# Expert weights in DMA rows of 16 KB, each transfer filling two neighbouring slots of the weight ring

## The reference

```python
logits = xf @ w_router + b_router                    # 32 experts
top_v, top_e = lax.top_k(logits, 4)
gates = softmax(top_v)
# for each expert e, for the tokens that chose it:
gu = xb @ w_e1[e] + b_e1[e]                          # w_e1[e]: 1024 x 2048
g, u = gu[:, :1024], gu[:, 1024:]
g = minimum(g, 7.0); u = clip(u, -7.0, 7.0)
h = (u + 1.0) * (g * sigmoid(1.702 * g))
y = h @ w_e2[e] + b_e2[e]                            # w_e2[e]: 1024 x 1024
# weighted by the gates and added to the token's row; then residual and final RMSNorm
```

## Time and profile before

| what | value |
|---|---|
| median of 3 runs | 1271.91 us (1271.19 to 1272.47) |
| the profiled execution's own time | 1270.08 us |
| its span, first to last instruction | 1267.8 us |
| mean granted TensorE clock | 0.979 |
| PE busy in the span | 1165.9 us (92%) |
| bytes moved in the span | 457.40 MB, mean 361 GB/s |

### The profile page before, as it was taken

One profiled execution on the slowest core, in us unless ns is written; L12 is line 12 of the kernel. 1 busy time (PEld: TensorE's weight loads), 2 busy tenths in 40 slices (PEclk: granted clock), 3 DMA queues, 4 the chain that ended last, 5 costly groups with the idle time before them and its releaser, 6 DMA issues.

```text
span 1267.8 us, 15137 instructions
## 1 busy us (share of the span) xinstructions
PE 1165.9 (92%) x5540; PEld 567.2 (45%) x5540; DVE 338.3 (27%) x820; ACT 182.1 (14%) x354; POOL 27.7 (2%) x54
## 2 busy tenths in 40 slices
PE   8999999698899999999989898989999999999896
PEld 6888888386333343333333333323332323233332
DVE  3795424614122122021212121211202021212123
ACT  3114213203010111111010101111010111010102
POOL 4000001100000000000000000000000000000000
PEclk9999999888999999999999999999999999999999
DMA  9398333993799999999999999999999999999994
GB/s 302 91 289 274 137 102 132 362 419 115 278 390 416 421 422 422 421 422 422 421 422 422 421 422 422 421 422 421 421 421 422 420 422 422 421 422 422 421 422 168
DMA packets 92741, 457.40 MB, mean 361 GB/s; under 512 B 7827, under 2 KB 36715, under 8 KB 44069
## 3 DMA queue, kind: packets, MB, share of 16 engines
q1 hardware_dynamic: 90768, 452.27, 88.8%
q10 hardware_dynamic: 1117, 3.04, 0.6%
q0 software_dynamic: 832, 1.76, 0.5%
HBM read 453.71 MB, written 3.81 MB: 361 GB/s over the span
## 4 chain that ended last, share of the span: by engine, by line
PE 51%; DMA 24%; SPq 14%; DVE 6%; issue 3%; ACT 2%; ACTq 0%; POOL 0%; DVEq 0%
DMA ring<-in_w_e 23%; PE ps L1539 15%; SPq L353 12%; PE ps L1559 12%; PE ps L1250 11%; PE ps L1269 3%; DVE ring L955 2%; PE ps L1501 1%; PE ps L1510 1%; PE ps L1549 1%; SPq L361 1%; PE ps L1453 1%; DVE mix L1106 1%; DVE mix L1109 1%; DVE mix L1103 1%
## 5 line engine op out<-in xcount | busy, mean ns | idle before, releaser
L1539 PE MATMUL ps<-ring,mix 128*64 128x512 f32 x2016 | 457.5, 598 | 28.9 <-DMA ring<-in_w_e 27.6
L1539 PEld LDWEIGHTS ps<-ring,mix 128*64 128x64 f32 x2016 | 134.1, 136 | 336.8 <-issue 234.8
L1559 PE MATMUL ps<-ring,mix 128*64 128x512 f32 x1024 | 235.1, 613 | 22.0 <-issue 11.0
L1103 DVE TENSOR_SCALAR mix<-ps 128x512 f32<-128x512 f32 x32 | 22.1, 692 | 606.7 <-PE ps L1539 606.7
L1559 PEld LDWEIGHTS ps<-ring,mix 128*64 128x64 f32 x1024 | 79.5, 140 | 156.0 <-issue 142.0
L686 ACT ACTIVATE mix<-mix 128x512 f32<-128x512 f32 x32 | 20.1, 630 | 420.3 <-DVE mix L1103 420.3
L1510 PEld LDWEIGHTS ps<-mix 128*128 128x128 f32 x544 | 65.5, 198 | 14.4 <-issue 13.0
L1510 PE MATMUL ps<-mix 128*128 128x128 f32 x544 | 70.1, 284 | 1.3 <-ACT rstd L668 1.3
L696 ACT ACTIVATE mix<-ps 64x512 f32<-64x512 f32 x64 | 37.8, 591 | 227.1 <-PE ps L1559 226.8
L1090 DVE SCALAR_TENSOR_TENSOR mix<-mix,gates 128x1024 f32<-128x1024 f32 x16 | 20.5, 1284 | 154.8 <-ACT mix L696 154.8
L1250 PE MATMUL ps<-mix,ring 128*128 128x264 f32 x256 | 60.2, 400 | 0.3 <-ACT mix L639 0.3
(11 more groups left out here) (294 smaller groups left out, 651.6 us busy)
## 6 DMA issues: line engine op xcount, KB each, us to landing
ring<-in_w_e SPq DMA_DIRECT2D x380, 1024.0 KB, 25.0
ring<-in_w_in SPq DMA_DIRECT2D x8, 1024.0 KB, 15.7
ring<-in_cache_mem_k SPq DMA_DIRECT2D x8, 1024.0 KB, 4.9
ring<-in_cache_mem_v SPq DMA_DIRECT2D x8, 1024.0 KB, 8.3
ring<-in_w_k SPq DMA_DIRECT2D x4, 1024.0 KB, 8.9
ring<-in_w_v SPq DMA_DIRECT2D x4, 1024.0 KB, 12.7
ring<-in_w_out SPq DMA_DIRECT2D x4, 1024.0 KB, 12.5
ring<-in_w_q SPq DMA_DIRECT2D x4, 1024.0 KB, 12.0
```

The source lines that it names most:

```text
L1103: dve.tensor_scalar(g1, ps[0][:, :], LIMIT, None, ALU.min).then_inc(S["g_clamped"], 1)
L1539: m = pe.matmul(ps[gu][CAP * i:CAP * i + CAP, :], xeT[:, k, CAP * e2:CAP * e2 + CAP], g_u[gu][:, 512 * i:512 * i + 512], start=False, stop ...
L1559: m = pe.matmul(ps[3][CAP * i:CAP * i + CAP, :], hTv[:, k % 4, CAP * (k // 4):CAP * (k // 4) + CAP], ring[:, s, D * (k % 2) + 512 * i:D * ...
```

## The change

Each transfer of expert weights now covers two neighbouring slots: 2 MB, 128 rows of 16 KB. To make a row of 16 KB out of `w_e1`, a partition takes two neighbouring rows of it (2p and 2p+1 of a block of 256), of which one comes to lie in slot s and the other in slot s+1; for `w_e2` it takes four. `fill` is called for every second slot and waits until both slots are freed; one semaphore, that of the even slot, stands for both. On the other side `DEAL[k]`, a slice with step 2, picks the token columns that match slot k, in `gather`, in the transposes of the sample tokens and in `fill_head`; `turn_h` picks every fourth column of h instead of every second. No arithmetic is added or taken away.

```diff
--- before.py
+++ after.py
@@ -76,6 +76,7 @@
 assert MOE0 % RING == 0
 HEAD_SLOTS = W_SLOTS // 2
 KC_SLOTS = 8
+DEAL = [slice(2 * P * (_k // 2) + _k % 2, 2 * P * (_k // 2 + 1), 2) for _k in range(KD)]
 
 
 IN_ORDER = [4, 5, 6, 7, 0, 1, 2, 3]
@@ -343,19 +344,18 @@
 
                 sp.wait_ge(S["freed"], free)
                 if s < W_SLOTS:
-                    src = a["w_e1"][0][bass.ds(e, 1), s * P:(s + 1) * P, :].rearrange("o p c -> p (o c)")
-                    dst = ring[:, s, :]
+                    src = a["w_e1"][0][bass.ds(e, 1), s * P:(s + 2) * P, :].rearrange("o (p t) c -> p (o t c)", t=2)
                 else:
                     j = s - W_SLOTS
-                    src = a["w_e2"][0][bass.ds(e, 1), j * 2 * P:(j + 1) * 2 * P, :].rearrange(
-                        "o (p t) c -> p (o t c)", t=2)
-                    dst = ring[:, s, :]
+                    src = a["w_e2"][0][bass.ds(e, 1), j * 2 * P:(j + 2) * 2 * P, :].rearrange(
+                        "o (p t) c -> p (o t c)", t=4)
+                dst = ring[:, s:s + 2, :].rearrange("p s c -> p (s c)")
                 sp.dma_start(dst, src).then_inc(filled[s], 16)
 
             def expert(e, b, first=0):
 
-                for s in range(first, RING):
-                    fill(e, s, RING * b + freed_after(MOE0 + s - RING))
+                for s in range(first, RING, 2):
+                    fill(e, s, RING * b + freed_after(MOE0 + s + 1 - RING))
 
             def bias(e):
                 sp.dma_start(b1q[0:97:32, :], a["b_e1"][0][bass.ds(e, 1), :].rearrange("o (g c) -> (o g) c", g=4)).then_inc(
@@ -363,7 +363,7 @@
 
             def fill_head(k):
                 for gu in range(2):
-                    sp.dma_start(head[k][gu], a["w_e1"][0, 0, k * P:(k + 1) * P, D * gu:D * gu + D]).then_inc(S["head_filled"], 16)
+                    sp.dma_start(head[k][gu], a["w_e1"][0, 0, DEAL[k], D * gu:D * gu + D]).then_inc(S["head_filled"], 16)
 
 
             sp.wait_ge(S["freed"], freed_after(KV_ENTRY[7]))
@@ -371,20 +371,20 @@
             sp.wait_ge(S["score_done"], H)
             fill_head(1)
             fill_head(2)
-            for s in range(HEAD_SLOTS, W_SLOTS):
-                fill(0, s, freed_after(MOE0 + s - RING))
+            for s in range(HEAD_SLOTS, W_SLOTS, 2):
+                fill(0, s, freed_after(MOE0 + s + 1 - RING))
             bias(0)
-            for s in range(HEAD_SLOTS):
-                fill(1, s, freed_after(MOE0 + s - RING))
-            for s in range(W_SLOTS, RING):
-                fill(0, s, freed_after(MOE0 + s - RING))
+            for s in range(0, HEAD_SLOTS, 2):
+                fill(1, s, freed_after(MOE0 + s + 1 - RING))
+            for s in range(W_SLOTS, RING, 2):
+                fill(0, s, freed_after(MOE0 + s + 1 - RING))
             sp.wait_ge(S["tm_turned"], 6)
             fill_head(3)
             sp.wait_ge(S["b1_used"], 1)
             bias(1)
 
-            for s in range(HEAD_SLOTS, W_SLOTS):
-                fill(1, s, freed_after(MOE0 + 2 * (s - HEAD_SLOTS)))
+            for s in range(HEAD_SLOTS, W_SLOTS, 2):
+                fill(1, s, freed_after(MOE0 + 2 * (s + 1 - HEAD_SLOTS)))
             expert(1, 1, W_SLOTS)
             with sp.Fori(2, NE) as e:
                 sp.wait_ge(S["b1_used"], e)
@@ -1507,7 +1507,7 @@
                 for i in halves:
                     for k in range(4 * i, 4 * i + 4):
                         for t in range(2):
-                            m = pe.matmul(ps[4 + i][:, P * (k % 4):P * (k % 4) + P], xnt[:, t, k * P:(k + 1) * P],
+                            m = pe.matmul(ps[4 + i][:, P * (k % 4):P * (k % 4) + P], xnt[:, t, DEAL[k]],
                                           sel[:, t, :], start=(t == 0), stop=(t == 1))
                 if halves[-1] == 1:
                     m.then_inc(S["gathered"], 1)
@@ -1531,9 +1531,9 @@
                         pe.wait_ge(S["head_filled"], 2 * 16 * HEAD_SLOTS)
                         g_u = head[k]
                     elif k < HEAD_SLOTS:
-                        pe.wait_ge(filled[k], 16 * b + 16 * (fills_before(MOE0 + k) - 1))
+                        pe.wait_ge(filled[k - k % 2], 16 * b + 16 * (fills_before(MOE0 + k) - 1))
                     else:
-                        pe.wait_ge(filled[k], 16 * b + 16 * fills_before(MOE0 + k))
+                        pe.wait_ge(filled[k - k % 2], 16 * b + 16 * fills_before(MOE0 + k))
                     for gu in range(2):
                         for i in range(2):
                             m = pe.matmul(ps[gu][CAP * i:CAP * i + CAP, :], xeT[:, k, CAP * e2:CAP * e2 + CAP],
@@ -1545,15 +1545,14 @@
             def turn_h(b):
                 pe.wait_ge(S["h_ready"], b + 1)
                 for j in range(4):
-                    c = 2 * P * (j // 2) + j % 2
-                    m = pe.transpose(ps[2][:, j * P:(j + 1) * P], hh[:, c:c + 2 * P - 1:2], ident[:, :])
+                    m = pe.transpose(ps[2][:, j * P:(j + 1) * P], hh[:, j:4 * P:4], ident[:, :])
                 m.then_inc(S["h_turned"], 1)
 
             def down(b):
                 pe.wait_ge(S["hT_ready"], b + 1)
                 for k in range(KD):
                     s = W_SLOTS + k // 2
-                    if k % 2 == 0:
+                    if k % 4 == 0:
                         pe.wait_ge(filled[s], 16 * b + 16 * fills_before(MOE0 + s))
                     for i in range(2):
                         m = pe.matmul(ps[3][CAP * i:CAP * i + CAP, :], hTv[:, k % 4, CAP * (k // 4):CAP * (k // 4) + CAP],
@@ -1600,7 +1599,7 @@
 
             pe.wait_ge(S["xnt_kept"], 6)
             for k in range(KD):
-                m = pe.transpose(ps[2][:, NB * k:NB * k + NB], xnt[0:NB, 2, k * P:(k + 1) * P], ident[0:NB, 0:NB])
+                m = pe.transpose(ps[2][:, NB * k:NB * k + NB], xnt[0:NB, 2, DEAL[k]], ident[0:NB, 0:NB])
             m.then_inc(S["smp_chain"], 1)
             pe.wait_ge(S["gt0_kept"], 1)
             gather(0)
```

## The result

| | before | after |
|---|---|---|
| median of 5 runs | 1271.19 us (1269.91 to 1272.47) | 1261.19 us (1260.38 to 1264.40) |
| the profiled execution's own time | 1270.08 us | 1263.79 us |
| its span | 1267.8 us | 1261.4 us |

The ratio is 0.9931, with a 95% interval from 0.9917 to 0.9944: 8.8 us less, 7.1 to 10.6 (the medians themselves are 10.0 apart). The forecast was 9.3 less, 1262.6.

What follows compares the result with a forecast made beforehand. The DMA engines, full from about 380 us, were taken as the bound, not PE. Rows -12.7, start +1.7 and end +1.7 gave -9.3 us, a median forecast of 1262.6 us, range 1258.5 to 1268.5.

Steps and rivals of the forecast that it cites:

- The price of a row: Full DMA stretch, experts 3 to 31: 9.1 ns per row and engine, 29.96 to 29.52 us an expert, -12.7 us.
- the stretches of 1 KB and 8 KB: Windows at 85 to 115 and 700 to 1200 us, 349 and 421 GB/s, giving 9.1 ns to a row.
- mixed windows of 4 KB: Value-cache and `w_o` stretch, 420 and 407 GB/s with another queue's packets; bounds the row at 0.7 to 10.7 ns.
- the small price: Rival: a row costs 5.7 ns or less; at 5.7, 7.9 us saved, 3.4 paid, 1267.4 us; chance 0.13.
- The messages: Completion messages at the end of each transfer, sent half as often; counted at nothing.
- The start: Last DMA pause, at `up` of expert 2, ends one step of `up` later, when slots 0 and 1 are free: +1.7 us.
- The pause: DMA engines run out before `up` of expert 2 frees slots: from 378.0 to the pair being free at 378.9.
- The end: Last expert: two steps of `up` instead of one follow the last landing, +1.7 us; `down` covered by 1.8 us.
- The operands: Larger load steps in `turn_h` (4 instead of 2) and `gather` (2 instead of 1): nothing, at most +0.8 us.
- The sum: Whole kernel: -12.7 + 1.7 + 1.7 = -9.3 us; profiled execution 1260.8 us, median 1262.6 us.
- no price, only grain: Rival: 421 GB/s is the ceiling for long rows, only the coarser grain is left, +3.4 us, 1275.3; chance 0.08.
- PE as the bound: Rival: PE takes over at 55.45 us to a pair; forecast 59.04 stays 3.6 above; no chance of its own given.

Runs made afterwards that it cites:

- e4_we2_4k: The kernel before with only the rows of `w_e2` cut to 4 KB, single-slot transfers; 1278.54 us against 1270.96, ratio 1.0059.
- e1_pair_8k: The change's transfers of two slots, but with rows of 8 KB and the layout of the kernel before; 1274.53 us against 1270.96, ratio 1.0027.
- e8_deal2: The kernel before with only the new layout of `w_e1`, single transfers and 8 KB rows; 1271.68 us against 1271.33, ratio 1.0006.
- e9_deal4: The kernel before with `w_e1` laid out by every fourth row, gather step 4, single transfers, 8 KB rows; 1281.87 us against 1271.33, ratio 1.0090.
- e5_we2_16k: The kernel before with only `w_e2` in pairs of slots and rows of 16 KB; 1266.87 us against 1270.96, ratio 0.9966.
- e2_quad_16k: The change with `w_e1` in transfers of four slots, rows still 16 KB; 1268.53 us against 1271.17 of before, ratio 0.9976.
- e3_quad_32k: The change with `w_e1` in transfers of four slots and rows of 32 KB, gather step 4; 1275.21 us against 1271.17 of before, ratio 1.0033.
- before_again: The kernel before, unchanged, profiled once more; 1270.99 us in one run.

## Why the prediction was right, step by step

**The price of a row** was the step on which all rested, and it held: 29.52 us forecast, 29.53, 29.51 and 29.52 in three profiles. The kernels in one table (rows per engine and expert, us per expert in the full stretch):

| kernel | rows | us |
|---|---|---|
| e4_we2_4k | 128 | 30.21 |
| before, e1_pair_8k, e8_deal2, e9_deal4 | 96 | 29.96, 29.97, 29.95, 29.97 |
| e5_we2_16k | 80 | 29.80 |
| after, e2_quad_16k | 48 | 29.53, 29.52 |
| e3_quad_32k | 32 | 29.35 |

From 128 rows to 32 it is 0.86 us, 9.0 ns to a row, and the single steps of the table give 8 to 11 ns. The 9.1 ns from the stretches of 1 KB and 8 KB were right. So was the term as a whole: e1_pair_8k and the change, which differ only in the rows and their layout, lie 12.6 us apart where it said 12.7, and e8_deal2 shows no price or gain of the layout. What in the engines or the memory takes the 9 ns no run tells. The 3.5 ns estimated from the 3 cycles of the Trainium skill, page "DMA: Bandwidth & Descriptors", section "Why small descriptors are slow (HBM only)", were too low by a factor of two and a half, for rows of 4 to 32 KB. The mixed windows of 4 KB, from which I took the rival "the small price", were no measure; e4_we2_4k was.

**The messages**, counted at nothing, are worth nothing that e1_pair_8k could show (29.97 with half of them).

**The start** was forecast at +1.7. The pause is there and ends with the pair. In the profile, though, the full stretch began 1.7 + 3.0 us later, since PE was late. This is the term that was mis-sized in the profiled execution: 29 x 0.43 = 12.5 less, 4.7 more at the start, which gives 7.8, and the last mark moved from 1239.47 to 1231.79, 7.7. What it costs in an execution without a profile isn't known; the total of e1_pair_8k, +3.6, leaves little room for more than the two steps. The pause itself can be told from the late PE by counting from the start of `up` of expert 2 to the last landing: 864.1 and 863.4 us in the two profiles of before, 866.2 in e1_pair_8k. The coarser grain costs 2.1 to 2.8 us there, somewhat more than the 1.7. In the three profiles of the change it is 853.3 to 853.4 us.

**The end** was forecast at +1.7 and measured at 3.68 - 1.96 = 1.72; `down` didn't wait.

**The operands**: `turn_h` with step 4 takes 207 ns to a load against 204, `gather` with step 2 200 against 198. I had left up to 0.8 us open for it; it was nothing. The two rows that I compared for the price of a step, 204 ns and 198, belong to two different instructions, though. With step 1 a load of `turn_h` takes 141 ns (e4_we2_4k), so there step 2 did have a price, and the kernel before was already paying it.

**The sum**: the profiled execution moved by -6.3 instead of -9.3, which is the late start. The medians moved by -10.0, -9.1 and -9.4 on three occasions. Profile against profile the gain is 6.3 to 8.3 us, since every profile of the change has the late start (in the 8.3 there is even a help of 1.7: the last `down` of before_again took 8.80 us instead of 7.10, with PEclk at 0.83 in 1240 to 1250 us). Why the medians show so little of the late start isn't known. The mechanism and its largest term are shown, but that the medians moved to within 1 us of the forecast is in part luck. One reading was slightly off: the earlier trace rows have 416 GB/s in the 13th slice and 420 to 422 from the 14th on, not 420 to 423, which changes nothing in the sum. Of the rivals, the one on the other side (no price, only grain) is what e1_pair_8k looks like, +3.6 us against the +3.4 computed. PE as the bound did not come with this change; e3_quad_32k shows how near it was.

## What to carry to other kernels

In a stretch where the DMA engines are never idle, take the price of a row from two long, pure stretches with different rows of the same profile, and not from short mixed ones; then multiply by the rows on one engine. Book the coarser grain at the two ends of the stretch, one step of the consumer each, and look at the pause before it and the last landing for them. Longer rows usually change a layout that somebody else reads: find that reader, and check its step before going further: a gain of 0.17 us to an expert in the transfers was lost to gathers that took 1.9 us longer each, most of it before the DMA engines were full.

## What was not expected of the hardware

A weight load of 128 x 128 floats takes 196 to 198 ns with step 1, 200 to 202 ns with step 2 and 328 to 329 ns with step 4 in `gather`. In `turn_h` it takes 141 ns with step 1, 204 to 205 ns with step 2 and 207 to 216 ns with step 4. The load with step 1 is from e4_we2_4k:

```profile
L1548 PEld LDWEIGHTS ps<-ident,mix 128*128 128x128 f32 x128 | 14.6, 141 | 29.3 <-DVE mix L1109 24.2 <-issue 5.1
```

So `gather` pays for the way from step 2 to 4 and `turn_h` for the one from step 1 to 2; no run tells why.

The low stretches of TensorE's granted clock between 295 and 375 us fall in one of two patterns in kernels whose work there is the same but for details: 0.50 in 300 to 305 us (before, before_again, e8_deal2), or 0.92 to 1.00 there and 0.66 to 0.76 in 295 to 300 us (the three profiles of the change, e1_pair_8k, e2_quad_16k, e4_we2_4k, e5_we2_16k). With the second pattern PE reaches the `up` of expert 2 between 1 and 3 us later than in the kernel before.
